# Feed-forward down with seven block products for eight in nine of eleven chunks, run between the next chunk's gate and up, with the weights' high parts made by ScalarE

## The reference

```
hn = rms_norm(x, g)
x = x + (silu(hn @ w_gate) * (hn @ w_up)) @ w_down      # 1024 x 2816, 1024 x 2816, 2816 x 1024
```

## Time and profile before

| | us |
|---|---|
| median of three runs | 2644.88 |
| profiled execution | 2652.98 |
| its span, first to last instruction | 2651.2 |
| TensorE busy in it | 2520.0 |
| GpSimd busy | 1295.5 |
| VectorE busy | 1364.3 |
| ScalarE busy | 746.3 |

### The profile page before, as it was taken

The page is one execution under the profiler, slowest core; times in us unless marked ns, Lnnn a source line. Parts: engine busy times, 40 slices in busy tenths (PEclk is TensorE's granted clock), DMA queues, the critical chain, the costliest instruction groups (busy, mean ns, idle before and its releaser), DMA issues. The chain is left out here.

```text
span 2651.2 us, 35441 instructions
## 1 busy us (share of the span) xinstructions
PE 2520.0 (95%) x11808; PEld 2081.7 (79%) x11808; DVE 1364.3 (51%) x2279; ACT 746.3 (28%) x1378; POOL 1295.5 (49%) x1020
## 2 busy tenths in 40 slices
PE   6999999999999999999879999999889999999997
PEld 5887888887788888888767777777767888888886
DVE  6215555557544343333766666676675344433336
ACT  3112111124211111111365555655642111111113
POOL 3323332223777777777311122221125877776776
PEclk9999999999999999999989999999989999999998
DMA  3323221211111111111100011111001111111111
GB/s 125 115 80 108 73 75 53 70 34 44 52 48 47 55 56 63 47 47 48 58 24 27 34 42 42 42 40 35 18 35 44 56 47 47 49 55 63 55 48 64
DMA packets 62730, 143.55 MB, mean 54 GB/s; under 512 B 6448, under 2 KB 16832, under 8 KB 59856
## 3 DMA queue, kind: packets, MB, share of 16 engines
q1 hardware_dynamic: 45136, 119.71, 13.8%
q10 hardware_dynamic: 17536, 23.07, 2.5%
HBM read 130.13 MB, written 12.63 MB: 54 GB/s over the span
## 5 line engine op out<-in xcount | busy, mean ns | idle before, releaser
L548 POOL TENSOR_SCALAR w_hi<-raw 128x1024 fp32r<-128x1024 f32 x80 | 89.7, 1121 | 863.3 <-PE bank L753 584.8
L581 POOL TENSOR_SCALAR a_hi<-raw_block 128x512 fp32r<-128x512 f32 x256 | 176.5, 689 | 391.1 <-PE bank L753 282.5
L1689 DVE TENSOR_TENSOR tmp<-bank,tmp 128x512 f32<-128x512 f32 x116 | 80.2, 692 | 544.7 <-PE bank L753 544.7
L584 POOL TENSOR_TENSOR a_lo<-raw_block,a_hi 128x512 fp32r<-128x512 f32 x256 | 349.2, 1364 | 20.5
L1306 ACT ACTIVATE tmp<-bank 128x512 f32<-128x512 f32 x116 | 69.6, 600 | 711.2 <-PE bank L753 711.2
L751 PE MATMUL bank<-T_hi,a_hi 128*128 128x512 f32 x672 | 261.8, 390 | 2.1 <-POOL a_hi L581 1.0
L753 PE MATMUL bank<-T_hi,a_lo 128*128 128x512 f32 x672 | 261.5, 389 | 0.0
L752 PE MATMUL bank<-T_lo,a_hi 128*128 128x512 f32 x672 | 261.5, 389 | 0.0
L751 PE MATMUL bank<-B_hi,a_hi 128*128 128x512 f32 x576 | 224.6, 390 | 0.0
L753 PE MATMUL bank<-B_hi,a_lo 128*128 128x512 f32 x576 | 224.2, 389 | 0.0
L752 PE MATMUL bank<-B_lo,a_hi 128*128 128x512 f32 x576 | 224.1, 389 | 0.0
(11 more groups left out here) (193 smaller groups left out, 6278.5 us busy)
## 6 DMA issues: line engine op xcount, KB each, us to landing
raw_block<-f_blocks_in SPq DMA_DIRECT2D x176, 256.0 KB, 2.6
raw<-w_units_in SPq DMA_DIRECT2D x80, 512.0 KB, 3.2
d_raw<-f_down_in SPq DMA_DIRECT2D x22, 1024.0 KB, 4.7
v_raw<-v_scratch ACTq DMA_DIRECT2D x16, 512.0 KB, 4.1
bias<-rel_scratch ACTq DMA_DIRECT2D x8, 640.0 KB, 3.7
x<-x_t_in SPq DMA_DIRECT2D x16, 256.0 KB, 6.6
v_scratch<-atmp ACTq DMA_DIRECT2D x16, 256.0 KB, 2.6
v_scratch<-full ACTq DMA_DIRECT2D x16, 256.0 KB, 2.5
```

Source lines behind the costliest of these rows:

```text
L548: pool.tensor_scalar(w_hi[slot][:, :], raw[r][:, :], 1.0, 1.0, ALU.mult, ALU.mult).then_inc(w_split, 1)
L581: pool.tensor_scalar(out, full, 1.0, 1.0, ALU.mult, ALU.mult).then_inc(made, 1)
L584: pool.tensor_tensor(out, full, r32(hi), ALU.subtract).then_inc(made, 1)
L1689: dve.tensor_tensor(dst, src[:, :], dst, ALU.add).then_inc(w.cadd, 1)
```

## The change

Chunks 1 to 9 (nine of the eleven) do down in Winograd's form too. The left side is the chunk's part of w_down, read as 2 x 2 blocks (A11, A12: two hidden tiles for the first four output tiles; A21, A22 for the last four), in 256 KB blocks through the same `raw_block` and the same slots as gate and up. The right side is the 2 x 2 blocks of the hidden tiles: B11, B21, B22 and T1 to T4 of them are made anew for every chunk. A block product of down is four output tiles of three matmuls, 84 matmuls in a chunk. Each product is read from its bank and added into x as soon as it is there, 28 adds; S2 accumulates upon A11 in banks 4 to 7, then S1 and S4, and A22 upon S3 in banks 0 to 3, each when the add two products earlier has read the bank.

Down of chunk i runs between gate and up of chunk i + 1. Chunk 1 therefore has gate and up alone, and chunk 9 ("late") is followed by its own down. Chunk 0 and chunk 10 keep their down.

The high parts of the weights of these groups are made by ScalarE (`left_high`), each behind the product that frees its slot. GpSimd makes 4 sums and 7 low parts a group (`middle_group`). ScalarE makes the high parts of the right side (`right_high`), VectorE its sums and low parts (`first_sums`, `last_sum`, `right_low`). Chunk 1's gate and both groups of the last chunk still have their high parts from GpSimd (`group`).

The diff, cut to its core:

```diff
+ORDER_G = ["A11", "A12", "S2", "S3", "S1", "S4", "A22"]
+ORDER_D = ["A11", "A12", "S2", "S3", "S1", "A22", "S4"]
+MID_HEAD = ["sum S1", "lo A11", "sum S3", "lo A12", "sum S2", "sum S4", "lo S2", "lo S3", "lo S1"]
+DOWN_TO = {"A11": (0, 0), "A12": (0, 0), "S2": (1, 0), "S3": (1, 1), "S1": (1, 1), "A22": (1, 0), "S4": (0, 1)}
+HI_ORDER = ["B11", "T1", "T3", "T2", "B22", "B21", "T4"]
...
 SyncE
+                def down_blocks(it, made):
+                    for op, f, half, b in (("lo S2", 0, 0, 0), ("lo S3", 0, 1, 2), ("lo S4", 1, 0, 1), ("lo A22", 1, 1, 3)):
+                        sp.wait_ge(s.made, made(op))
+                        down_block(it, f, half, b)
+                def chunk(it):
+                    gate_up(it, 0, lambda op: middle(it, AT_G0 - 1, MID, MID_MADE + MID_G[op]), after_g)
+                    down_blocks(it - 1, lambda op: middle(it, AT_G0, MID, MID_MADE + MID_G[op]))
+                    gate_up(it, 1, lambda op: middle(it, AT_D, MID, MID_MADE + MID_D[op]), after_d)
...
 GpSimd
+                def middle_group(it, at, down):
...
+                    def low_part(op, b_, before):
+                        slot = order.index(op)
+                        pool.wait_ge(s.left_hi, middle(it, at, 7, slot + 1))
+                        after(before)
+                        low(lo[slot], b_, hi[slot], s.made)
+                    loaded(2)
+                    loaded(3)
+                    after(None)
+                    pool.tensor_tensor(s1_sum[:, :], b[2], b[3], ALU.add).then_inc(s.made, 1)
+                    low_part("A11", b[0], "sum S1")
+                    pool.tensor_tensor(b[2], b[0], b[2], ALU.subtract).then_inc(s.made, 1)
+                    low_part("A12", b[1], "sum S3")
+                    pool.tensor_tensor(b[0], s1_sum[:, :], b[0], ALU.subtract).then_inc(s.made, 1)
+                    pool.tensor_tensor(b[1], b[1], b[0], ALU.subtract).then_inc(s.made, 1)
+                    low_part("S2", b[0], "sum S4")
+                    low_part("S3", b[2], "lo S2")
+                    low_part("S1", s1_sum[:, :], "lo S3")
...
 TensorE
+                def down_products(it, late):
+                    for pos, op in enumerate(ORDER_D):
+                        pe.wait_ge(s.made, made(op))
+                        pe.wait_ge(s.t_lo, (7 * (LATE - 1) if late else it * 7 - 14) + (pos + 1))
...
+                        upper = op in ("A11", "S2", "S1", "S4")
+                        for n in range(4):
+                            if pos > 1:
+                                pe.wait_ge(s.d_added, base + (4 * (pos - 2) + n + 1))
+                            product(bank[4 + n if upper else n][:, :], (a_hi[pos][:, cols], a_lo[pos][:, cols]),
+                                    (right_hi_of(DOWN_RIGHT[op]), right_lo_of(DOWN_RIGHT[op])), ...)
...
                         for g in range(2):
+                            if g == 1 and kind != "second":
+                                down_products(it, False)
+                                pe.wait_ge(s.d_added, down_base(it, False) + (4 * 5 + 4))
...
-                        down(it, None, 1, 0, ((1, 2), (0, 3)))
-                        down(it, None, 0, 8, ((0, 1), (1, 4)))
+                        if kind == "late":
+                            down_products(it, True)
...
 ScalarE, a chunk from the second on
+                        right_high(it - 1, "B21")
+                        right_high(it - 1, "T4")
                     product(0, "A11")
+                    snap(bank[0], gated[0])
+                    behind_gate(0)
+                    behind_gate(1)
                     product(0, "S2")
+                    snap(bank[0], gated[1])
+                    silu(gated[0][:, :], gated[0])
+                    behind_gate(2)
                     product(0, "S1")
+                    snap(bank[0], gated[2])
+                    behind_gate(3)
+                    behind_gate(4)
+                    silu(gated[2][:, :], gated[2])
                     product(0, "S4")
+                    silu(bank[0][:, :], gated[3])
+                    behind_gate(5)
+                    behind_gate(6)
+                    silu(gated[1][:, :], gated[1])
+                        for pos in range(7):
+                            act.wait_ge(w.d_prod, down_base(it, False) + 4 * (pos + 1))
+                            left_high(it, AT_G1, False, pos)
                     product(1, "A11")
+                    snap(bank[2], hidden_part(h_full, 0, 0))
+                    behind_up(0)
+                    behind_up(1)
                     product(1, "S2")
+                    snap(bank[2], hidden_part(h_full, 1, 0))
+                    behind_up(2)
                     product(1, "S1")
+                    snap(bank[2], hidden_part(h_full, 1, 1))
+                    behind_up(3)
+                    behind_up(4)
+                    right_high(it, "B11")
+                    behind_up(5)
+                    for name in ("T1", "T3", "T2", "B22"):
+                        right_high(it, name)
+                    behind_up(6)
...
 VectorE
+                def first_sums(it):
+                    dve.tensor_tensor(right_full("T1"), b12, b11, ALU.subtract).then_inc(w.t_full, 1)
+                    dve.tensor_tensor(right_full("T3"), b22, b12, ALU.subtract).then_inc(w.t_full, 1)
+                    dve.tensor_tensor(right_full("T2"), b22, right_full("T1"), ALU.subtract).then_inc(w.t_full, 1)
+                    right_low(it, "B11", 1)
+                def last_sum(it):
+                    dve.wait_ge(w.full, it * 4 + 4)
+                    dve.tensor_tensor(right_full("T4"), hidden_part(h_full, 1, 0), right_full("T2"), ALU.subtract
+                    right_low(it, "B21", 4)
+                    right_low(it, "T2", 4)
...
+                        last_sum(it - 1)
+                        right_low(it - 1, "T3")
+                        right_low(it - 1, "T1", 3)
                     product(0, "A12")
                     snap(1)
+                    cadd(gated[0][:, :], bank[1])
+                        right_low(it - 1, "T4")
+                        right_low(it - 1, "B22", 3)
```

More of the change, by code:

```diff
@@ L83, with middle, chunks @@
                                                (0, "S4"), (1, "S4")])}
+ORDER_G = ["A11", "A12", "S2", "S3", "S1", "S4", "A22"]
+ORDER_D = ["A11", "A12", "S2", "S3", "S1", "A22", "S4"]
+MID_HEAD = ["sum S1", "lo A11", "sum S3", "lo A12", "sum S2", "sum S4", "lo S2", "lo S3", "lo S1"]
+MID_G = {op: n + 1 for n, op in enumerate(MID_HEAD + ["lo S4", "lo A22"])}
+MID_D = {op: n + 1 for n, op in enumerate(MID_HEAD + ["lo A22", "lo S4"])}
+MID = len(MID_G)
+MID_MADE = 20 + GROUP
+DOWN_RIGHT = {"A11": "B11", "A12": "B21", "S2": "T2", "S3": "T3", "S1": "T1", "A22": "T4", "S4": "B22"}
+DOWN_TO = {"A11": (0, 0), "A12": (0, 0), "S2": (1, 0), "S3": (1, 1), "S1": (1, 1), "A22": (1, 0), "S4": (0, 1)}
+HI_ORDER = ["B11", "T1", "T3", "T2", "B22", "B21", "T4"]
+D_SUMS = 28
+LATE = CHUNKS - 2
+AT_G0, AT_D, AT_G1, AT_D_LATE = -5, -4, -3, -2
+def middle(it, at, per, i):
+    return it * (3 * per) + (at * per + i)
+def chunks(eng, body):
+    body(0, "first")
+    body(1, "second")
+    with eng.Fori(2, LATE) as it:
+        body(it, "middle")
+    body(LATE, "late")
+    body(CHUNKS - 1, "last")
 class Count:
@@ L672, in group, with chunk @@
                     low(lo[6], b[3], hi[6], s.made)
-                def chunk(it, first, last):
-                    if first:
+                def chunk(it, kind):
+                    if kind == "first":
                         if name == "F1":
@@ L704, in chunk @@
[L704 to L705 removed]
+                        pool.wait_ge(s.prod, N_PROD.at(it, PROD_LAST[0, op]))
+                    loads = 4 + 3 * LATE + AT_D_LATE
+                    group(loads + 1, lambda op: MADE_LAST + MADE[op], free_first)
+                    group(loads + 2, lambda op: MADE_LAST + LAST[op], free_second, tail=False)
+                    down(2, [MADE_LAST + LAST[f"hi d{f}"] for f in range(2)])
@@ L964, in first_chunk, with one @@
                     down(0, "first", 1, 8, ((0, 3), (1, 4)))
-                def one(it, first, last):
-                    if first:
+                def one(it, kind):
+                    if kind == "first":
                         first_chunk()
@@ L971, in made @@
                     def made(g, op):
-                        pe.wait_ge(s.made, N_MADE.at(it, LAST[op] if last and g else g * GROUP + MADE[op]))
+                        if kind == "last":
+                            pe.wait_ge(s.made, MADE_LAST + (LAST[op] if g else MADE[op]))
+                        elif kind == "second" and g == 0:
+                            pe.wait_ge(s.made, MADE_SECOND + MADE[op])
+                        else:
+                            pe.wait_ge(s.made, middle(it, AT_G1 if g else AT_G0, MID, MID_MADE + MID_G[op]))
                     def snap(i):
@@ L1384, in last_chunk, with one @@
                     std(n + 1, 1)
```

(31 more changed lines are left out.)

271 lines of the change are left out of this document (180 added, 91 removed).

## The result

The changed kernel takes 2681.74 us, the median of four runs (2675.48 to 2684.74), for 2644.57 (2643.95 to 2647.23) of the kernel before on the same chip: ratio 1.0136, 95% interval 1.0116 to 1.0155. It is slower by 37 us. The forecast was 2666, in a range of 2618 to 2684.

A forecast was written before the change was run, and what follows sets the result against it. TensorE, busy 95% of the span, was taken as the bound. Per part +6.0 us in chunks, +2.5 and +2.3 at the ends gave +10.8, both +21.6: 2674.6, on the median's scale 2666 us, range 2618 to 2684.

The forecast's parts named there:

- the gain of 2.72 us a chunk: Down in nine chunks: 84 matmuls for 96 save 2.72 us a chunk, 49 us in all, if TensorE never waits.
- Adds at the products' pace: VectorE's 28 adds into x during down, one per 0.68 us of matmuls, were costed at nothing.
- Rival C: VectorE's adds bound down at 0.83 us each, 4 us a chunk more: 2730 us; chance 0.08 with anything worse.
- The ring: Middle chunks: ScalarE highs, GpSimd lows, loads and sums delay bank copies; 3.4 + 0.1 us of waits, 60.6 us a chunk.
- rival A: Middle chunks: waits shrink to those without VectorE-GpSimd port waits, 57.9 us a chunk, 2623 us; chance 0.17.
- The first wait is a part of the second: Middle chunks' gate: 1.7 us late before S2, 3.4 in all before S4, including the first, not added to it.
- Rival B: Middle chunks' gate: first wait as reckoned, second falls within it; 58.9 us a chunk, 2639 us; chance 0.17.
- The ends: First and last chunks of each feed-forward part: +2.5 us up to the last gate and +2.3 in the last chunk.
- "+2.5" to the last gate: Chunk 1's gate and chunk 9's down: 2.15 + 3.6 + 0.1, less 2.72 and 0.6, a part.
- "+2.3" behind it: Last chunk of each part: late weight blocks and low parts from GpSimd cost 2.3 us.
- rival D: TensorE's clock may drop behind new waits; counted as nothing because they are short; no chance of its own.
- From the profiled execution to the median: Whole kernel: the profiled 2652.98 us lay 8.1 above the median, so 2674.6 became 2666 us.

The follow-up runs named there:

- e7: Changed kernel with two ScalarE bank copies ahead of high parts, VectorE's bank add ahead of two lows, and one copy moved in chunk 1; 2626.1 us, ratio 0.9914.
- e12: The changed kernel run once more without any edit; 2680.2 us, ratio 1.0127.
- e4: Changed kernel with VectorE's sums T1, T3 and T2 taking their first operand from a PSUM bank instead of SBUF; 2652.4 us, ratio 1.0022.
- e5: Changed kernel with ScalarE making the high of A22 ahead of the highs of T1, T3, T2 and B22; 2695.69 us, ratio 1.017.
- e1: Changed kernel with ScalarE's copy of gate's first bank ahead of its highs of B21 and T4; 2694.0 us, ratio 1.0184.
- e2: Changed kernel with ScalarE's copy of S1's bank ahead of its high of S2, in gate and up; 2643.09 us, ratio 0.9982.
- e9: e1 with six more matmuls, their result unread, ahead of the wait before S4 in gate; 2677.56 us, ratio 1.0117.
- e6: Changed kernel with GpSimd making all high parts of the middle groups' weights and ScalarE none; 2882.54 us, ratio 1.0884.

## Why the prediction was right, and where it was short

1. *TensorE is the bound, and only new waits can spoil the gain of 2.72 us a chunk.* Right; e7 shows 57.45 with no wait.
2. *Adds at the products' pace.* Right in the middle chunks: 0.68 us each, no wait in down. Rival C is out.
3. *The ring.* Right in each step of the table to 0.3 us, with both waits at their places for ScalarE's copies and 60.70 us a chunk for 60.6 (60.82 in F2, 60.84 in e12). The profile calls the waits 1.11 and 1.70; each block of 12 then starts late by 0.16 more (a matmul lasts 0.39 and the next would have started 0.23 after it) and restarts with 0.11 lost: 1.4 + 2.0 = 3.4. The rule of the Trainium skill's page "SBUF — State Buffer", section "Who interferes with whom", on which rival A hung, is borne out in this kernel by e4 (0.69 for 1.27 with one operand in a bank) and e5 (three lows in 4.06 for 1.89 beside GpSimd).
4. *The first wait is a part of the second.* Right: e1 moved it, and of the two orders only e2's took time away by itself. Rival B is what e2 comes to from the other side: 58.6 to 58.9 in six of eight periods, for its 58.9.
5. *The ends*, "+2.5" to the last gate and "+2.3" behind it: mis-sized. Measured in F1 are +9.4 (16.2 from the first mark to the last chunk's, less 8 x 0.85 in the chunks) and +1.1. Of the 6.9 us missed before the last gate half, 3.45, are in chunk 1's gate. By the forecast S4 starts 13.7 us after the first copy there; in e12 it does so after 13.8, and its gate is 1.8 longer than the forecast by the clock alone. In the profiled execution it starts after 15.6, since GpSimd lay later: 1.9, and 1.5 for the clock. The other half is in chunk 9. There the first wait is as forecast (2.43, for the low of B11 at 2.5). The step that failed is what comes behind it: the sum had one more wait of 1.0, for the low of B21, and nothing for VectorE, whose adds into x stand behind right-side low parts. The waits for those adds are 1.44 + 0.43 here, with 1.8 us of slow clock over them, and 1.07 + 1.75 + 0.45 at full clock in e9. In the last chunk the waits for low S3 (1.50 for 1.4) and for d_lo (1.35, as before) are there, the one of 1.0 for low A11 is not.
6. *The clock*, rival D: "the new waits are of the short kind, so I count nothing". Right in the middle, wrong at the ends, where it fell twice a part. The fall in chunk 1 is 1.5 us a part, 3 of the 15.7 us between 2666 and 2681.74; the one in chunk 9 costs at most 0.6 us by e9. The rows for it were at hand: the earlier trace rows had a stretch with long waits at 0.95, and my own reckoning had waits of 2.15 plus 0.6 in chunk 1. I weighed the clock for the chunk's waits alone.
7. *From the profiled execution to the median* by subtracting 8.1: it held to 3 us (34.5 in the parts, 37 between the medians).

That 2681.74 lies inside the range of 2618 to 2684 is luck in part. Its upper end stood for chunks of 61.6 us; the chunks took 60.7 to 60.8, and most of the 15.7 us come from the ends, for which the range had no room of its own.

## What to carry to other kernels

An engine that works in order and serves the bound should do the short thing that the bound waits for before anything that can itself be late; here one call moved behind another, in two places, turns 1.4% slower into 0.2% faster, and four such moves make it 0.9% faster. Follow such a ring through every queue, load and port, in time, before and after the change: it gave the period to 0.1 to 0.2 us. Put the ends of a loop and what the clock does behind their longer waits into the sum as terms of their own, ask of each loss whether it only covers another wait, and take nothing from an engine's idle time before looking at who uses it.

## What the runs showed that I had not expected

- The clock may fall to half behind a wait of 2.3 us and may not: 2.34 in e1 with clock 0.50 and matmuls of 0.6 us and more behind it, 2.33 in the chunk before, in the same execution, without. It fell behind 2.43, 2.91 and 3.88; it never fell behind the 1.1 and 1.7 of the changed kernel's middle chunks, and it held behind 2.42 in e9 and 2.54 in e2. In e6, with many waits close together, it fell behind waits of 1.8 and held behind one of 3.24. So the length of the last wait alone does not decide; what does was not settled.
- A fall takes 1.5 to 1.7 us of TensorE's pace, and that is time only where nothing else would have been waited for: 1.5 us in e1's chunks, at most 0.6 in chunk 9.
- Six useless matmuls in each such wait make e1 faster by 16 us.
- A VectorE operation with one operand in a bank runs at full speed beside GpSimd (0.69), so the place of an operand decides over more than its own length: 29 us of the kernel for three operations a chunk (e4).
- Taking idle time from GpSimd made the kernel slower (e5, 1.017 for 1.0136), though the ring that I had followed started earlier.
